# A transformer layer with 32 experts: order of the last weight loads, a rebuilt end, plain activations

## The chip, the cores and the metric
The kernel runs on one core of a Trainium2 chip. The metric is the device time of one execution in microseconds (us). TensorE (PE in the profile), VectorE (DVE), ScalarE (ACT) and GpSimd (POOL) compute; SyncE (SP) does no arithmetic here, it issues nearly all the transfers from the chip's memory.

## The reference
Input x is 256 tokens by 1024, all float32. The layer is

```
mix = three attention groups of x, projected        # first 195 us, not touched by the change
x   = layer_norm(2**0.25 * x + mix) * ln1_g + ln1_b
logits = x @ router_w + router_b ; the 4 best of 32 experts per token, softmax weights w
for each expert e, for its tokens t:
    gu   = x[t] @ w_gate_up[e] + b_gate_up[e]        # 1024 x 2048
    gate = min(gu[:, :1024], 7) ; up = clip(gu[:, 1024:], -7, 7)
    act  = gate * sigmoid(1.702 * gate) * (up + 1)
    ffn[t] += w * (act @ w_down[e] + b_down[e])      # 1024 x 1024
out = layer_norm(2**0.25 * x + ffn) * ln2_g + ln2_b
```

## The kernel before
Every expert's weights are read once: 8 MB for gate and up ("gu") and 4 MB for down ("dn"). SBUF holds two gu buffers (`gu_slot`, one for even experts, one for odd) and one dn buffer (`dn_slot`). A gu is loaded in four chunks of 2 MB, a dn in four of 1 MB. An expert has 64 slots for its tokens. If more tokens chose it, a block of 32 extra slots is run through the same weights (`extra_blocks`). With this input that happens for experts 1 and 15, one block each.

TensorE handles the experts in order. For expert n: 32 gate-up matmuls and 4 for the bias into banks PB4 and PB5 (`gate_up`); then, beside VectorE, the gathering of the next two experts' tokens (after an odd n) or the combine of the last two experts' outputs (`combine`, after an even n); four transposes of `act_sb` (`act_transposes`); 16 down matmuls (`down`). `combine` is a matmul of `CT` (one-hot rows times routing weight, transposed) with `ysb` (outputs of two experts), and adds into banks PB0 to PB3.

VectorE turns gate and up into the activation (`activations`, L1632 to L1638): a minimum and a clip out of PSUM, one multiply with add, a wait for ScalarE's sigmoid, one multiply. The clip results are written interleaved (`by_rows`), since row p of the down weights in SBUF holds four neighbouring rows of the matrix. After the activation VectorE loads the count of extra blocks (`first_extra_slots`, L1682) and, where it is above 0, makes the one-hots of the extra slots (L1656, L1658), for which TensorE waits in `extra_gather`.

The loads stand in one queue, in the order of SyncE's program, and run in that order. SyncE issues chunk c of gu(n+2) when gate-up chunk c of expert n is done (semaphore `guc`, and `xguc` for extra blocks), and chunk c of dn(n+1) when down chunk c of expert n is done (`dn_used`). In the loop (L415) step n issues gu(n+2) and then dn(n+1). For n = 28 and 29 (L423) the two stand the other way round: dn(n+1), then gu(n+2). Last comes dn(31), then ln2_g and ln2_b (L434).

At the end (L1253) TensorE runs gate-up 31, the transposes, down 31 and one combine for experts 30 and 31. Then VectorE, for each half of the tokens (b = 0, 1): residual sum out of PSUM (L1741), statistics (L1513), two normalising passes (L1530, L1535), while GpSimd makes the reciprocal deviation (L520). SyncE writes 128 tokens (512 KB) with one transfer.

Of the kernel before, what the change touches and what calls it, by code (L numbers as in the profile page):

```python
# [22 lines left out]
PAIRS = N_EXPERTS // 2  # L23
SLOTS = 64
# [32 lines left out]
def hybrid_layer(nc, x, w_in, b_in, pos_k, pos_v, w1_k, w2_k, w1_v, w2_v, g_out, w_out, ln1_g, ln1_b,  # L57
                 router_w, router_b, w_gu, b_gu, w_dn, b_dn, ln2_g, ln2_b, out):
    with ExitStack() as ctx:
# [82 lines left out]
        fg, fb = reg_a[:, 0:D], reg_a[:, D:2 * D]  # L142
# [172 lines left out]
        def _(sp_):  # L315
# [98 lines left out]

            with sp.Fori(0, PAIRS - 2) as i:  # L415
                for par in range(2):

                    count_extra_blocks(2 * i + par)
                    next_gu(i, par)
                    next_dn(i, par)  # L420


            for par in range(2):  # L423
                count_extra_blocks(N_EXPERTS - 4 + par)
                next_dn(PAIRS - 2, par)
                next_gu(PAIRS - 2, par)
# [11 lines left out]
            sp.wait_ge(s["outd"], 16 * TB)  # L438
# [92 lines left out]
        def _(act):  # L531
# [205 lines left out]
            sigmoid(1)  # L737
            act_columns(5, 1)
            combine_weights(1)
            act.wait_ge(s["nx_ok"], 1)  # L740
            extra_blocks(0)
            expert_output(0, 1)
            with act.Fori(0, PAIRS - 1) as i:
                sigmoid(2 * i + 2)
                slots_to_sbuf(0, 6, 2 * i + 3)
                act_columns(5, 2 * i + 2)
                slots_to_sbuf(1, 4, 2 * i + 4)
                extra_blocks(2 * i + 1)
                expert_output(1, 2 * i + 2)
                sigmoid(2 * i + 3)  # L750
                act_columns(5, 2 * i + 3)
                combine_weights(i + 2)
                extra_blocks(2 * i + 2)
                expert_output(0, 2 * i + 3)
            sigmoid(N_EXPERTS)
            act_columns(5, N_EXPERTS)
            extra_blocks(N_EXPERTS - 1)
            expert_output(1, N_EXPERTS)
# [3 lines left out]
        def _(pe):  # L762
            mm_, tr = pe.matmul, pe.transpose

# [454 lines left out]
            clear_outputs()  # L1219
            pe.wait_ge(s["ysb_ok"], 1)  # L1220
# [4 lines left out]
            extra_blocks(0, 1, 0, "ct_sb", 1, 0)  # L1225
# [38 lines left out]
        def _(dve):  # L1264
# [455 lines left out]
            with dve.Fori(0, PAIRS - 1) as i:  # L1720
                expert_activations(2 * i + 2)
                next_expert_rows(0, 2 * i + 1)
                first_extra_slots(2 * i + 1)
                extra_blocks(2 * i + 1, 2 * i + 2)
                expert_output(1, 2 * i + 2)
                expert_activations(2 * i + 3)
                next_expert_rows(1, 2 * i + 2)
                first_extra_slots(2 * i + 2)
                extra_blocks(2 * i + 2, 2 * i + 3)
                next_one_hots(i + 1)  # L1730
                expert_output(0, 2 * i + 3)
            expert_activations(N_EXPERTS)
            first_extra_slots(N_EXPERTS - 1)
            extra_blocks(N_EXPERTS - 1, N_EXPERTS)
            expert_output(1, N_EXPERTS)

            dve.wait_ge(s["comb"], PAIRS + 1)
            for b in range(TB):
                for h in range(2):
                    c = slice(512 * h, 512 * h + 512)  # L1740
                    ins = stt(in_order(yf[:, b, c]), by_rows(x_sb[:, b, c]), ALPHA, in_order(PB[2 * b + h][:, :]), ALU.mult,  # L1741
                              ALU.add)
                link(ins)
                half_stats(yf, b, 0)
                link(half_stats(yf, b, 1))
                for h, ins in enumerate(norm(yf, b, TB + b + 1, fg, fb, yf, "ln2_ld")):
                    if h == 1:
                        ins.then_inc(s["fout"], 1)
# [28 lines left out]
```

## Time and profile before

| | us |
|---|---|
| median of 3 runs (lowest, highest) | 1178.83 (1178.04, 1180.24) |
| the profiled execution, its own time | 1177.09 |
| its span, first to last instruction | 1174.9 |
| busy: PE | 1070.8 |
| busy: DVE | 290.6 |
| busy: ACT | 147.7 |
| read from memory | 424.91 MB, mean 363 GB/s |

The profile is of one execution. Its own time is 2.2 us more than its span. Shares of the span say little here, since TensorE and the transfers are both nearly always busy from 285 us on: which of the two is waited for has to be read stretch by stretch. TensorE's granted clock is 1.00 where the engine has its full 2.4 GHz and 0.50 at 1.2 GHz. A float32 matmul is recorded as two matmul entries, so 96 entries are the 16 down and 32 gate-up matmuls that follow each other. "SPq" rows are SyncE's transfer issues.

### The profile page before, as it was taken

To read this page: it belongs to the slowest core of one execution; us is meant where nothing else is said; L and a number is where in the kernel's file an instruction comes from. 1 tells how busy PE (TensorE), PEld (TensorE's weight loads), DVE (VectorE), ACT (ScalarE), POOL (GpSimd) and SP (SyncE) were. 2 spreads that over 40 slices of the span, in tenths; PEclk is the share of its full clock that TensorE was granted. 3 is DMA by queue.
4 is the path that set the end of the run, shared out by engine and by line. 5 is a ranking of instruction groups with operands and counts; after the bars stand their busy time and mean duration, and the time that the engine had idled before them with its cause. 6 is when DMAs were issued, how large, how long until landed. Compare 5 with 4: busy or idle time off the path is not lost.

```text
span 1174.9 us, 14685 instructions
## 1 busy us (share of the span) xinstructions
PE 1070.8 (91%) x5364; PEld 461.1 (39%) x5365; DVE 290.6 (25%) x770; ACT 147.7 (13%) x313; POOL 29.2 (2%) x54
## 2 busy tenths in 40 slices
PE   7999898788999999999999879999999999999984
PEld 6777544332343433323232323434343333333331
DVE  2354654221212121221212212121212121212224
ACT  2043511110010111101010100101010100010100
POOL 3001300000000000000000000000000000000000
PEclk9999997888999999999999989999999999999997
DMA  9723439829999999999999989999999999999980
GB/s 310 269 88 72 184 153 399 343 90 377 426 427 426 427 426 426 427 426 427 426 426 426 426 351 423 426 426 427 426 427 426 427 427 428 424 427 424 426 337 36
DMA packets 48980, 426.32 MB, mean 363 GB/s; under 512 B 5033, under 2 KB 8922, under 8 KB 16154
## 3 DMA queue, kind: packets, MB, share of 16 engines
q1 hardware_dynamic: 48378, 425.37, 87.6%
q10 hardware_dynamic: 576, 0.61, 0.2%
q8 instruction: 16, 0.26, 0.1%
q14 instruction: 10, 0.08, 0.0%
HBM read 424.91 MB, written 1.05 MB: 363 GB/s over the span
## 4 chain that ended last, share of the span: by engine, by line
PE 59%; DMA 29%; DVE 9%; issue 2%; SPq 1%; ACT 1%; DVEq 0%
PE PB L766 57%; DMA WB<-in_w_down_dram 28%; DVE S L1632 2%; DVE S L1633 2%; DVE S L1635 1%; DVE S L1638 1%; PE PB L1123 1%; DMA WB<-in_w_in_dram 1%; DVE S L1530 0%; DVE K L1513 0%; DVE S L1741 0%; DVE S L1496 0%; SPq L330 0%; DVE WB L1415 0%; DVE S L1658 0%
## 5 line engine op out<-in xcount | busy, mean ns | idle before, releaser
L766 PE MATMUL PB<-WB,S 128*64 128x512 f32 (+5 forms) x3456 | 758.4, 595 | 30.8 <-DMA WB<-in_w_down_dram 21.4
L766 PEld LDWEIGHTS PB<-WB,S 128*64 128x64 f32 (+2 forms) x3456 | 255.6, 140 | 513.6 <-issue 440.2
L1632 DVE TENSOR_SCALAR S<-PB 128x512 f32<-128x512 f32 (+1 forms) x34 | 35.5, 1045 | 478.6 <-PE PB L766 478.6
L766 PE MATMUL PB<-S 32*64 32x512 f32 (+5 forms) x464 | 108.1, 586 | 3.2 <-ACT S L700 1.4
L1676 DVE COPY S<-PB 64x512 f32<-64x512 f32 x32 | 21.9, 684 | 264.9 <-PE PB L766 264.9
L704 ACT ACTIVATE S<-S 128x512 f32<-128x512 f32 x32 | 20.2, 630 | 473.0 <-DVE S L1632 473.0
L766 PE MATMUL PB<-S,X 128*128 128x128 f32 x512 | 66.1, 284 | 1.0 <-DVE S L1574 1.0
L766 PEld LDWEIGHTS PB<-S,X 128*128 128x128 f32 x512 | 61.8, 198 | 13.3 <-issue 12.2
L766 PE MATMUL PB<-S,WB 128*128 128x256 f32 (+2 forms) x336 | 60.2, 377 | 1.0 <-ACT S L542 0.5
L766 PEld LDWEIGHTS PB<-S 32*64 32x64 f32 (+5 forms) x464 | 33.1, 147 | 65.2 <-issue 58.0
L766 PEld LDWEIGHTS PB<-S,WB 128*128 128x128 f32 (+1 forms) x336 | 46.5, 170 | 12.3 <-issue 2.1
L720 ACT ACTIVATE S<-PB 64x512 f32<-64x512 f32 x32 | 19.0, 594 | 255.0 <-PE PB L766 255.0
L766 PE MATMUL PB<-WB 128*32 128x128 f32 (+8 forms) x276 | 45.9, 353 | 4.4 <-DVE WB L1461 2.8
L1123 PE MATMUL PB<-K,S 128*128 128x128 f32 x128 | 21.4, 290 | 24.6 <-DVE S L1638 24.6
L766 PEld LDWEIGHTS PB<-WB 128*64 128x64 f32 (+2 forms) x276 | 29.4, 152 | 16.4 <-issue 12.2
L1633 DVE TENSOR_SCALAR S<-PB 128x512 f32<-128x512 f32 (+1 forms) x34 | 35.8, 1053 | 0.1
L1123 PEld LDWEIGHTS PB<-K,S 128*128 128x128 f32 x128 | 13.8, 143 | 41.2 <-DVE S L1638 36.3
L520 POOL TENSOR_TENSOR K<-K 128x1 f32<-128x1 f32 x4 | 3.9, 984 | 997.4 <-DVE K L1526 997.4
L708 ACT ACTIVATE S<-PB 128x512 f32<-128x512 f32 x32 | 19.1, 597 | 66.0 <-PE PB L1123 66.0
L1635 DVE SCALAR_TENSOR_TENSOR S<-S 128x512 f32<-128x512 f32 (+1 forms) x34 | 23.5, 691 | 1.2
L1638 DVE TENSOR_TENSOR S<-S 128x512 f32<-128x512 f32 (+1 forms) x34 | 23.5, 691 | 1.2
L668 ACT ACTIVATE S<-PB 128x512 f32<-128x512 f32 x32 | 19.1, 597 | 15.2 <-PE PB L766 15.2
(208 smaller groups left out, 345.9 us busy)
## 6 DMA issues: line engine op xcount, KB each, us to landing
WB<-in_w_gate_up_dram SPq DMA_DIRECT2D x128, 2048.0 KB, 23.9
WB<-in_w_down_dram SPq DMA_DIRECT2D x128, 1024.0 KB, 21.7
WB<-in_w_in_dram SPq DMA_DIRECT2D x3, 2048.0 KB, 15.8
WB<-in_w_in_dram SPq DMA_DIRECT2D x1, 2144.0 KB, 10.9
WB<-in_w_in_dram SPq DMA_DIRECT2D x2, 1024.0 KB, 10.6
WB<-in_w_out_dram SPq DMA_DIRECT2D x2, 1024.0 KB, 9.7
WB<-in_w_out_dram SPq DMA_DIRECT2D x1, 2048.0 KB, 7.9
WB<-in_w_in_dram SPq DMA_DIRECT2D x1, 1040.0 KB, 12.7
```

What stands on the lines that cost most here:

```text
L520: pool.tensor_tensor(st[:, o + 2:o + 3], st[:, o + 1:o + 2], half[:, 0:1], ALU.pow).then_inc(s["lnp"], 1)
L668: act.activation(xg[:, 4 * h:4 * h + 4, :].rearrange("p k s -> p (k s)"), PB[bank][:, :], ACT.Copy)\
L704: act.activation(act_sb, gt, ACT.Sigmoid, scale=SWIGLU_ALPHA).then_inc(s["sig"], 1)
L708: act.activation(actT[:, :, :].rearrange("p c s -> p (c s)"), PB[bank][:, :], ACT.Copy)\
L720: act.activation(ysb[64 * e:64 * e + 64, 1, :], PB[7][64:128, :], ACT.Copy).then_inc(s["ysb_ok"], 1)
L766: return mm_(o, l, r, start=start, stop=stop, skip_group_check=True)
L1123: ins = tr(PB[5][:, P * c:P * c + P], act_sb[:, P * c:P * c + P], ident)
L1632: ts(by_rows(g), in_order(gate), LIMIT, None, ALU.min).then_inc(s[g_ok], 1)
L1633: ts(by_rows(u), in_order(up), LIMIT, -LIMIT, ALU.min, ALU.max).then_inc(s[clip], 1)
L1635: stt(u, u, 1.0, g, ALU.add, ALU.mult).then_inc(s[upg], 1)
L1638: tt(a, u, a, ALU.mult).then_inc(s[done], 1)
L1676: cp(ysb[64 * e:64 * e + 64, 0, :], PB[7][0:64, :]).then_inc(s["ysb_dv"], 1)
```

## The change
- **Order of loads.** `IN_ORDER = 3`: the order dn(n+1), gu(n+2) begins at n = 24 instead of n = 28.
- **Activations.** The minimum and the clip read PSUM and write SBUF in plain order. The interleaving moves into the transposes: `every_fourth` picks columns m, m+4, m+8, ... of `act_sb` as the matrix to be transposed. It is the operand that is loaded as weights (LDWEIGHTS).
- **Extra slots.** `first_extra_slots(n)` stands before `expert_activations(n+1)` on VectorE. (On TensorE and ScalarE the extra block of expert 0 moves ahead of the first combine; with this input it is empty.)
- **End on TensorE.** In gate-up 31, the outputs of expert 30 are added after chunks 0 and 1 (K = 64 rows), and the combine weights of expert 31 are transposed after chunk 2. After the bias, four matmuls with the identity add 2**0.25 * x (which ScalarE has written out as `x_plain`) into PB0 to PB3. After down 31 the last combine has K = 64 rows: upper and lower rows hold the two halves of the 1024 columns.
- **End on VectorE and SyncE.** Statistics and the first normalising pass read PSUM; both halves' statistics come first, then both norms. Each 128 tokens by 512 columns (256 KB) is written when it is ready.

```diff
-            with sp.Fori(0, PAIRS - 2) as i:
+            with sp.Fori(0, PAIRS - 1 - IN_ORDER) as i:
...
-            for par in range(2):
-                count_extra_blocks(N_EXPERTS - 4 + par)
-                next_dn(PAIRS - 2, par)
-                next_gu(PAIRS - 2, par)
+            with sp.Fori(PAIRS - 1 - IN_ORDER, PAIRS - 1) as i:
+                for par in range(2):
+                    count_extra_blocks(2 * i + par)
+                    next_dn(i, par)
+                    next_gu(i, par)
...
             for b in range(TB):
-                sp.wait_ge(s["fout"], b + 1)
-                sp.dma_start(out[0, P * b:P * b + P, :], yf[:, b, :]).then_inc(s["outd"], 16)
+                for h in range(2):
+                    sp.wait_ge(s["fout"], 2 * b + h + 1)
+                    sp.dma_start(out[0, P * b:P * b + P, 512 * h:512 * h + 512], yf[:, b, 512 * h:512 * h + 512])\
+                      .then_inc(s["outd"], 16)
...
+                    act.activation(x_plain[:, b, c].rearrange("p (q m) -> p q m", q=P),
+                                   x_sb[:, b, c].rearrange("p (m q) -> p q m", q=P), ACT.Copy, scale=ALPHA)\
+                       .then_inc(s["xa"], 1)
+            act.wait_ge(s["ct"], PAIRS + 1)
+            act.activation(CT_last[:, :, :].rearrange("p b t -> p (b t)"), PB[6][:, 0:256], ACT.Copy).then_inc(s["ct_sb"], 1)
...
+            def every_fourth(a, m):
+                return a.rearrange("p (q m) -> p m q", m=4)[:, m, :]
...
-                    ins = tr(PB[5][:, P * c:P * c + P], act_sb[:, P * c:P * c + P], ident)
+                    ins = tr(PB[5][:, P * c:P * c + P], every_fourth(act_sb, c), ident)
...
-            gate_up(1, PAIRS, N_EXPERTS)
-            pe.wait_ge(s["ct_sb"], PAIRS)
+            def outputs_of_30(b):
+                for h in range(2):
+                    mm(acc(b, h)[:, :], CT[0:64, b, :], ysb[0:64, h, :], False, False)
...
+            for c in range(GU_CHUNKS):
+                pe.wait_ge(s_gul[1][c], 16 * PAIRS)
+                gate_up_chunk(c, 1).then_inc(s["guc"], 1)
+                if c == 0:
+                    pe.wait_ge(s["ysb_ok"], N_EXPERTS)
+                    pe.wait_ge(s["ysb_dv"], N_EXPERTS - 1)
+                if c < 2:
+                    outputs_of_30(c)
+                if c == 2:
+                    last_weight_transposes()
+            pe.wait_ge(s["oht"], N_EXPERTS)
+            gate_up_bias(1).then_inc(s["gu"], 1)
+            pe.wait_ge(s["xa"], 1 + 2 * TB)
+            for b in range(TB):
+                for h in range(2):
+                    mm(acc(b, h)[:, :], ident, x_plain[:, b, 512 * h:512 * h + 512], False, False)
...
-            combine()
+            for b in range(TB):
+                for h in range(2):
+                    mm(acc(b, h)[:, :], CT_last[64 * h:64 * h + 64, b, :], y_last[64 * h:64 * h + 64, :], False, True)\
+                        .then_inc(s["comb"], 1)
...
-                ts(by_rows(g), in_order(gate), LIMIT, None, ALU.min).then_inc(s[g_ok], 1)
-                ts(by_rows(u), in_order(up), LIMIT, -LIMIT, ALU.min, ALU.max).then_inc(s[clip], 1)
+                ts(g, gate, LIMIT, None, ALU.min).then_inc(s[g_ok], 1)
+                ts(u, up, LIMIT, -LIMIT, ALU.min, ALU.max).then_inc(s[clip], 1)
...
+                for h in range(2):
+                    dve.wait_ge(s["comb"], PAIRS + 1 + 2 * b + h)
+                    ins = dve.bn_stats(st[:, 12 * b + 6 * h:12 * b + 6 * h + 6], PB[2 * b + h][:, :])
...
+                    ins = stt(yf[:, b, c], PB[2 * b + h][:, :], st[:, o:o + 1], fg[:, c], ALU.subtract, ALU.mult)
...
+                    stt(yf[:, b, c], yf[:, b, c], st[:, o + 2:o + 3], fb[:, c], ALU.mult, ALU.add).then_inc(s["fout"], 1)
```

What this makes of the order, at three places. First SyncE inside the second half of a loop step: before, with a load of gu (L347) after its wait (L405), then dn (L352) after L412, as in every step up to 27:

```order
L347 DMA WB<-in_w_gate_up_dram 128x4096
L361 ISA
L405 ISA
L347 ISA
L347 DMA WB<-in_w_gate_up_dram 128x4096
L412 ISA
L352 ISA
L352 DMA WB<-in_w_down_dram 128x2048
```

and in the changed kernel in steps 24 to 29:

```order
L359 DMA WB<-in_w_down_dram 128x2048
L368 ISA
L419 ISA
L359 ISA
L359 DMA WB<-in_w_down_dram 128x2048
L412 ISA
L354 ISA
L354 DMA WB<-in_w_gate_up_dram 128x4096
```

The four chunks of dn(n+1) now come ahead of the four of gu(n+2) for four more values of n.

Second, VectorE in the loop, second expert of a step: the activation, the next expert's rows, then the count of extra blocks (nx):

```order
L1676 COPY S<-PB 64x512
L1671 REGISTER_ALU
L1632 TENSOR_SCALAR S<-PB 128x128x4
L1633 TENSOR_SCALAR S<-PB 128x128x4
L1635 SCALAR_TENSOR_TENSOR S<-S 128x512
L1638 TENSOR_TENSOR S<-S 128x512
L1615 TENSOR_SCALAR K<-K 128x1
L1611 TENSOR_SCALAR S<-K 128x64
L1679 REGISTER_ALU
L1679 TENSOR_LOAD nx
```

In the changed kernel the end of the one-hots of the extra slots, then the activation:

```order
L1714 TENSOR_SCALAR S<-K 128x32
L1716 TENSOR_SCALAR S<-K 128x32 x4
L1714 TENSOR_SCALAR S<-K 128x32
L1716 TENSOR_SCALAR S<-K 128x32 x4
L1744 UNCONDITIONAL_BRANCH
L1729 REGISTER_ALU
L1690 TENSOR_SCALAR S<-PB 128x512
L1691 TENSOR_SCALAR S<-PB 128x512
L1693 SCALAR_TENSOR_TENSOR S<-S 128x512
L1696 TENSOR_TENSOR S<-S 128x512
L1674 TENSOR_SCALAR K<-K 128x1
L1670 TENSOR_SCALAR S<-K 128x64
```

The one-hots have moved ahead of the wait for the gate-up matmuls, and the two PSUM readers have lost the 128x4 form.

Third, TensorE in expert 31, from its gate-up to the load of the count:

```order
L766 MATMUL PB<-WB,S 64x512 x32
L766 MATMUL PB<-S 64x512 x4
L1123 MATMUL PB<-K,S 128x128 x4
L1191 TENSOR_LOAD nx
L1191 ISA x2
```

and now:

```order
L791 MATMUL PB<-WB,S 64x512 x8
L791 MATMUL PB<-S 128x512 x2
L791 MATMUL PB<-WB,S 64x512 x8
L791 MATMUL PB<-S 128x512 x2
L791 MATMUL PB<-WB,S 64x512 x8
L1288 MATMUL PB<-K,WB 128x128 x2
L791 MATMUL PB<-WB,S 64x512 x8
L791 MATMUL PB<-S 64x512 x4
L791 MATMUL PB<-WB,K 128x512 x4
L1148 MATMUL PB<-K,S 128x128 x4
L1216 TENSOR_LOAD nx
```

Ten instructions stand before the four transposes that did not: four for expert 30, two transposes, four for the residual.

## Rows read from the trace of the kernel before

**Rows 1.** The page's part 2, 40 equal slices of the span.
```profile
GB/s 310 269 88 72 184 153 399 343 90 377 426 427 426 427 426 426 427 426 427 426 426 426 426 351 423 426 426 427 426 427 426 427 427 428 424 427 424 426 337 36
```

**Rows 2.** The chain of waits: start us, us, what.
```profile
1039.86 1.96 PE PB L766 x8
...
1069.41 16.73 PE PB L766 x80
```

**Rows 3.** The timeline, expert 30: start, us, engine, line, operation, [idle before <-releaser].
```profile
1113.02 1.04 DVE L1632 TENSOR_SCALAR S<-PB 128x512 f32<-128x512 f32 x1 [14.09 <-PE PB L766]
...
1116.46 0.66 PE L1123 MATMUL PB<-K,S 128*128 128x128 f32 x4 [0.74 <-DVE S L1638]
...
1118.13 20.82 PE L766 MATMUL PB<-WB,S 128*64 128x512 f32 x96
```

**Rows 4.** The timeline, SyncE's issues of dn(29) and of dn(31).
```profile
1064.09 7.71 SPq L352 DMA_DIRECT2D WB<-in_w_down_dram  x4
...
1120.20 5.47 SPq L352 DMA_DIRECT2D WB<-in_w_down_dram  x4
```

**Rows 5.** Stretches near the end; last columns: granted clock, DMA share, GB/s.
```profile
1135.00:1140.00 5.00, 4.97 (x28) 1.27 (x24) 0.00 (x0) 0.00 (x0) 0.00 (x0) 1.00 0.95 386
...
1145.00:1150.00 5.00, 4.70 (x14) 1.47 (x16) 0.00 (x0) 0.25 (x1) 0.00 (x0) 0.57 0.02 3
```

**Rows 6.** The timeline, expert 31 and the end.
```profile
1143.53 1.08 PE L1123 MATMUL PB<-K,S 128*128 128x128 f32 x4 [3.57 <-DVE S L1638]
...
1145.31 9.06 PE L766 MATMUL PB<-WB,S 128*64 128x512 f32 x32 [0.69 <-ACT S L708]
...
1155.25 3.67 PE L766 MATMUL PB<-S 128*128 128x512 f32 x8 [0.88 <-DVE S L1676]
...
1158.96 1.96 DVE L1741 SCALAR_TENSOR_TENSOR S<-X,PB 128x512 f32<-128x512 f32 x2 [3.85 <-PE PB L766]
1160.95 1.29 DVE L1513 BATCH_NORM_STATS2 K<-S 128x6 f32<-128x512 f32 x2
...
1162.59 1.40 DVE L1530 SCALAR_TENSOR_TENSOR S<-S,K,WB 128x512 f32<-128x512 f32 x2
...
1165.47 6.73 SPq L437 DMA_DIRECT2D out_dram<-S  x2
...
1170.42 1.41 DVE L1535 SCALAR_TENSOR_TENSOR S<-S,K,WB 128x512 f32<-128x512 f32 x2
```

**Rows 7.** The timeline, extra blocks of expert 1 (first two rows) and of expert 15.
```profile
256.69 9.62 PE L766 MATMUL PB<-WB,S 128*32 128x512 f32 x64 [0.47 <-ACT S L683]
...
278.51 1.99 PE L766 MATMUL PB<-S 64*128 64x512 f32 x8 [0.71 <-ACT S L700]
...
673.12 0.60 ACT L668 ACTIVATE S<-PB 128x512 f32<-128x512 f32 x1 [0.30 <-PE PB L766]
...
675.28 1.07 PE L766 MATMUL PB<-X,S 128*32 128x256 f32 x16 [2.19 <-DVE S L1658]
...
677.76 7.07 PE L766 MATMUL PB<-WB,S 128*32 128x512 f32 x64 [0.47 <-ACT S L683]
...
689.57 0.69 PE L1175 MATMUL PB<-K,S 128*128 128x128 f32 x2 [3.74 <-DVE S L1638]
```

**Rows 8.** Stretches of 6 us around the two extra blocks.
```profile
282.00:288.00 6.00, 6.00 (x30) 2.01 (x28) 0.44 (x1) 0.44 (x1) 0.00 (x0) 1.00 0.75 221
...
676.00:682.00 6.00, 5.02 (x50) 1.53 (x46) 0.00 (x0) 0.77 (x2) 0.00 (x0) 1.00 0.68 244
...
700.00:706.00 6.00, 6.00 (x30) 2.01 (x28) 0.00 (x0) 0.00 (x0) 0.00 (x0) 1.00 0.69 231
```

**Rows 9.** Groups by line and form (VectorE, 280 to 1140 us), and the page's part 5.
```profile
L1632 DVE TENSOR_SCALAR S<-PB 128x512 f32<-128x512 f32 x29 | 30.4, 1047 | 408.5 <-PE PB L766 408.5
...
L1676 DVE COPY S<-PB 64x512 f32<-64x512 f32 x30 | 20.5, 684 | 239.8 <-PE PB L766 239.8
...
L1123 PEld LDWEIGHTS PB<-K,S 128*128 128x128 f32 x128 | 13.8, 143 | 41.2 <-DVE S L1638 36.3
```

More of the change, by code:

```diff
@@ L141, in hybrid_layer @@
         yf = S2[:, 0:TB * D].rearrange("p (b d) -> p b d", b=TB)
-        fg, fb = reg_a[:, 0:D], reg_a[:, D:2 * D]
+        take = carver(reg_a)
+        fg, fb = take(D), take(D)
+        x_plain = take(TB * D, b=TB, d=D)
+        y_last = take(512)
+        CT_last = take(TB * P, b=TB, t=P)
+        ohw_last = take(TB * P, b=TB, s=P)
         K = sb("K", 1202)
@@ L757, in _ @@
             extra_blocks(N_EXPERTS - 1)
-            expert_output(1, N_EXPERTS)
+            act.wait_ge(s["dn_used"], N_EXPERTS * DN_CHUNKS)
+            act.activation(y_last[64:128, :], PB[7][64:128, :], ACT.Copy).then_inc(s["ysb_ok"], 1)
         @block.tensor
@@ L1251, in _, with last_weight_transposes @@
                 down(0, i + 2, 2 * i + 3)
[L1253 to L1254 removed]
+            def outputs_of_30(b):
+                for h in range(2):
+                    mm(acc(b, h)[:, :], CT[0:64, b, :], ysb[0:64, h, :], False, False)
+            def last_weight_transposes():
+                pe.wait_ge(s["ohs"], PAIRS + 2)
+                pe.wait_ge(s["ct_sb"], PAIRS)
+                for b in range(TB):
+                    ins = tr(PB[6][:, P * b:P * b + P], ohw_last[:, b, :], ident)
+                ins.then_inc(s["ct"], 1)
+            for c in range(GU_CHUNKS):
[11 more added lines that the diff above has]
+            pe.wait_ge(s["xa"], 1 + 2 * TB)
+            for b in range(TB):
+                for h in range(2):
+                    mm(acc(b, h)[:, :], ident, x_plain[:, b, 512 * h:512 * h + 512], False, False)
+            pe.wait_ge(s["ct_sb"], PAIRS + 1)
             act_transposes(N_EXPERTS)
@@ L1259, in _ @@
             pe.wait_ge(s["ysb_dv"], N_EXPERTS)
-            combine()
+            for b in range(TB):
+                for h in range(2):
+                    mm(acc(b, h)[:, :], CT_last[64 * h:64 * h + 64, b, :], y_last[64 * h:64 * h + 64, :], False, True)\
+                        .then_inc(s["comb"], 1)
         @block.vector
@@ L1731, in _ @@
                 expert_output(0, 2 * i + 3)
+            t = N_EXPERTS - 1
+            for b in range(TB):
+                for j in range(2):
+                    ins = ts(ohw_last[:, b, 64 * j:64 * j + 64], iota_s, posm[:, t, b:b + 1], wts[:, t, b:b + 1], ALU.is_equal,
+                             ALU.mult)
+            ins.then_inc(s["ohs"], 1)
+            first_extra_slots(t)
             expert_activations(N_EXPERTS)
[L1733 to L1737, printed above, removed]
+            extra_blocks(t, N_EXPERTS)
+            dve.wait_ge(s["dn_used"], N_EXPERTS * DN_CHUNKS)
+            cp(y_last[0:64, :], PB[7][0:64, :]).then_inc(s["ysb_dv"], 1)
             for b in range(TB):
+                o = 24 + 4 * b
+                for h in range(2):
+                    dve.wait_ge(s["comb"], PAIRS + 1 + 2 * b + h)
+                    ins = dve.bn_stats(st[:, 12 * b + 6 * h:12 * b + 6 * h + 6], PB[2 * b + h][:, :])
+                link(ins)
+                link(dve.bn_aggr(st[:, o:o + 2], st[:, 12 * b:12 * b + 12]))
+                ts(st[:, o + 1:o + 2], st[:, o + 1:o + 2], LN_EPS, None, ALU.add).then_inc(s["lnstat"], 1)
+            dve.wait_ge(s["ln2_ld"], 32)
+            for b in range(TB):
+                o = 24 + 4 * b
                 for h in range(2):
                     c = slice(512 * h, 512 * h + 512)
-                    ins = stt(in_order(yf[:, b, c]), by_rows(x_sb[:, b, c]), ALPHA, in_order(PB[2 * b + h][:, :]), ALU.mult,
-                              ALU.add)
+                    ins = stt(yf[:, b, c], PB[2 * b + h][:, :], st[:, o:o + 1], fg[:, c], ALU.subtract, ALU.mult)
                 link(ins)
[L1744 to L1748, printed above, removed]
+                dve.wait_ge(s["lnp"], TB + b + 1)
+                for h in range(2):
+                    c = slice(512 * h, 512 * h + 512)
+                    stt(yf[:, b, c], yf[:, b, c], st[:, o + 2:o + 3], fb[:, c], ALU.mult, ALU.add).then_inc(s["fout"], 1)
     return nc
```

18 lines of the change are left out of this document (10 added, 8 removed).

## The prediction, made before the changed kernel ran

> **What bounds the kernel now.** I read four views, in this order. The 40 slices first [rows 1]: the transfers run at 426 or 427 GB/s nearly everywhere from slice 10 on. One slice is lower (351, from 675 us), and slice 8 (from 235 us) has 90. So the weight stream is full, with gaps at two places.
>
> The chain of waits next: between 476 and 651 us, and between 896 and 1069 us, it is a row of transfers, one expert every 29.5 us (1039.86 to 1069.41 [rows 2]). From 1069.41 on it is TensorE and VectorE. An expert then takes 27.1 us (transposes at 1116.46 [rows 3], the next at 1143.53 [rows 6]). Three such experts lie between 1069.41 and the end of down 31 at 1154.4, so 1069.41 is the last chunk of dn(28).
>
> SyncE's issues and the stretches tell why [rows 4, 5]. dn(31) is issued at 1120.2, but the stream still moves 386 GB/s until 1140: what is left after 1069.41 (dn 29, gu 30, dn 30, gu 31, dn 31) is 29.4 MB, or 69 us at 427 GB/s. dn(31) has landed near 1138, down 31 ends at 1154.4. The load order of the loop brings gu(n+2) ahead of dn(n+1), which is needed first; when the stream ends, TensorE is 16 us behind it.
>
> The last view is the timeline of the end [rows 6]: from down 31's end at 1154.4 to the end of the span at 1174.9 are 20.5 us, nearly all on VectorE.
>
> **The order of the loads.** At 427 GB/s a gu takes 19.67 us (4.92 a chunk), a dn 9.84 (2.46 a chunk). dn(24) landed at 1069.4 - 4 x 29.52 = 951.3. Now seven dn and six gu follow in order of use: dn(31) lands at 951.3 + 68.9 + 118.0 = 1138.2, as before, gu(31) 9.8 before that, at 1128.4, and gu(30) 29.5 earlier, at 1098.9. From the last chunk of its gu to the end of its down, TensorE needs: 0.2 to start (an estimate), one gate-up chunk 3.46 (20.82 / 6, by 16 of 96 entries [rows 3]), bias 1.1, the wait for the activation 2.8 (next part), transposes and what follows until down 1.67 (1116.46 to 1118.13 [rows 3]), down 6.9 (20.82 / 3). That is 16.1. So down 30 ends at 1098.9 + 16.1 = 1115.0 (1125 before).
>
> Does the stream run dry? dn(n+1) is issued while down n runs; ahead of it then stands gu(n+1), up to 19.7 us long. Where before changes its order, dn(29) was issued from 1064.1 on [rows 4] with only dn(28) ahead of it, and no gap shows in the chain. At n = 24 TensorE also waits for the stream, so it is the same transition. I take no gap. The order would cost something only if TensorE were more than about 15 us behind there.
>
> Expert 31: four chunks 13.8; two times two matmuls for expert 30, which share their rows of the array and so don't pair: 4 x 0.86 = 3.4 (3.67 for four of full height [rows 6], 1.99 for four in pairs [rows 7]: both ends kept); two transposes 0.3; bias 1.1: 1115.0 + 18.6 = 1133.6. Then the residual, 3.5 by the same row. It fills the 3.57 us for which TensorE waited here [rows 6]; VectorE's chain (2.8) ends before it. Transposes and ScalarE's copy 1.35: 1138.4. Down 31 took 9.06 for 32 entries after that idle wait, with the clock at 0.57 [rows 5], against 6.9 at 1.00. With no idle wait I take 6.9 (9.1 is the other end). Down 31 ends at 1145.4, not 1154.4: **-9.0** (-6.5 to -10.5). ScalarE's four residual copies and the copy of the weights have 18 us before they are needed.
>
> **The activations.** L1632 takes 1047 ns, a plain copy out of PSUM 684 [rows 9]. Two of them: 0.72 us less per expert, so 2.8 instead of 3.5. TensorE waits 0.74 there [rows 3]; most of that goes, and then its gather or combine (2.8 to 2.9) is what lasts. In the stretches bound by transfers this is worth nothing. It counts in the 2.8 above and in the extra blocks.
>
> The other side is the transposes: their weight loads (143 ns each, four per expert [rows 9]) now read every fourth float32. No row of before shows a strided weight load. Below: nothing. Above: VectorE's scattered form costs (1047 - 684) / 512 = 0.7 ns per element, which on 128 columns is 0.09 us per load, 0.36 per expert. I take 0.2 per expert, and as the far end four times the load, 1.7 per expert. In transfer-bound stretches 0.2 is hidden; at the end it costs **+0.2**.
>
> Against this stands a rule of the Trainium skill, "Advanced Engine Details and Errata", section on memory cachelines: SBUF has lines of 16 bytes, and an access that goes to a new line each time pays. Every fourth float32 is exactly a new line. It gives no price, so it moves only the chance of the first rival; L1632 agrees in direction with its 1.5 times, if writes behave as reads.
>
> **The extra blocks** are where gaps in the stream can be closed. For expert 15 TensorE waits 2.19 us for the one-hots until 675.28 [rows 7]. Now they are made before gate-up ends. What is late next is ScalarE's copy of bank PB4, which starts at the gather's end and takes 0.60; the gather ends 0.6 earlier. It would end at 673.1, so 2.2 earlier than 675.28. Within the block TensorE waits 3.74 for an activation with two scattered reads [rows 7]: 0.7 less. That is 2.9, less 0.4 for strided transposes. The clock is a further term: the 64 entries took 9.62 in expert 1 and 7.07 in expert 15 [rows 7], so up to 2.5 in the first, and up to 2 in each after the long wait. I take 2.0 for expert 1 and 0.7 for expert 15.
>
> Does the stream gain it? gu(17) is held up by the extra gate-up, dn(16) by down 15. The two stretches lack (427 - 244) x 6 / 427 = 2.6 and 2.8 us [rows 8], so 5.4 at most; I take 3.2. For expert 1 the stretch 282 to 288 lacks 2.9 and restarts when down 1 does; the stream before it (gu 3) restarts 2.2 or more earlier too, so the cap is above 5. I take 4.5. After both gaps the stream is full, so all later landings move: **-7.7** (-5 to -10.3).
>
> **The tail.** After down 31: copies 0.85 (1154.4 to 1155.25). Combine in pairs 1.99 instead of 3.67; the first pair is done at half. Statistics start at 2.0 after down's end: 1.3 for two [rows 6], from PSUM the same I assume, then 0.4 to the next pass (1160.95 + 1.29 to 1162.6); for both halves of the tokens 5.5. Four pairs of passes: 1.45 out of PSUM, 1.4 the others: 5.7, so 11.2. GpSimd's step of the first half is hidden beside the second's statistics. Before, this was 17.4 (1171.83). The two residual passes of 1.96 and the last half's wait are what goes. The last transfer is 256 KB instead of 512; from VectorE's end to the span's end were 3.1 us, I take 3.0. Tail 14.2 instead of 20.5: **-6.3** (-5.3 to -7.3).
>
> **Sum.** Span 1174.9 - 9.0 + 0.2 - 7.7 - 6.3 = 1152.1. The profiled execution's own time would be 1177.09 - 22.8 = 1154.3, and the median of the runs, 1.7 above it, 1178.83 - 22.8 = **1156.0**.
>
> **Rivals.**
> - *Dear strided loads.* At 1.7 us per expert TensorE needs 27.9 per expert, still less than the stream's 29.5. But the lag of the extra blocks is barely paid back by expert 24, and each late expert adds. I worked it through expert by expert: 18 us worse, 1174. At 1.0 it is 5 worse, 1161. The skill's rule speaks for it, the nearest row (0.36) against it.
> - *The extra blocks give nothing* (the gaps stay, because the requests come no earlier than the stream's restart): 1163.7. Against it: both gaps end about 2 us after requests that hang on the extra block.
> - *The new order gives nothing*: TensorE waits in gate-up instead of in down, and a gap opens since dn(25) is issued late: 1165. Against it: dn(29) [rows 4] did the same without a gap.
> - *Slower than before.* The same strided loads, priced above 1.85 per expert, or 0.6 us for a load that took 0.14. Then TensorE is still behind at expert 24, and in the new order dn(25) isn't even asked for until down 24 runs, while nothing stands behind dn(24): the stream stops for 6 to 10 us there. At 2.1 per expert: 32 worse than the forecast, 1188.
> - *The two last gains overlap with something not seen*, leaving the time as it was: nothing in the rows speaks for it.
>
> **Chances.** Forecast 0.72; extra blocks nothing 0.09; order nothing 0.08; dear loads but still faster 0.06; no change 0.02; slower 0.03. A measurement of this kernel can tell about 0.2% (2.4 us) from no change. Faster 0.95, within 0.2% 0.02, slower 0.03. The ends of the terms give 1151 to 1161 for the forecast alone; the range for 8 in 10 is 1151.5 to 1164.5, which takes in the second rival.
>
> **What would show it.** In the changed profile: down 31's 32 entries take 6.9 at clock 1.00 and end near 1138; transfers end near 1131; the chain's waits for dn end at expert 24 and turn into short waits for gu chunks. The transposes' four entries stay near 0.66, weight loads near 0.14 to 0.23. The stretches at 676 and 700 us lack less than half of what they lacked. VectorE takes 11 us from down 31 to its last pass. The prediction is wrong if the transposes take over 2 us per expert, if the stream shows a gap after dn(24), or if down 31 still starts over 15 us after gu(31) has landed.

## The result, and the profile of the changed kernel

| | before | changed |
|---|---|---|
| median of four runs each | 1178.52 us (1178.04 to 1180.24) | 1150.92 us (1150.05 to 1152.26) |
| ratio, 95% interval | | 0.9765 (0.9747 to 0.9784) |
| profiled execution: own time, span | 1177.09, 1174.9 | 1150.07, 1147.9 |
| span until down 1 starts | 280.4 | 271.0 |
| last chunk of dn(24) landed | 951.3 | 938.9 |
| down 31 ends | 1154.4 | 1134.5 |
| from there to the end of the span | 20.5 | 13.4 |

The forecast was 1156.0 with a range of 1151.5 to 1164.5. The kernel came out 27.6 us faster, where 22.8 were forecast, and 0.6 us below the range.

The slices of the changed kernel, which answer to [rows 1]:

```profile
GB/s 309 263 110 74 148 132 395 400 149 399 423 426 425 427 427 426 427 427 425 427 427 425 429 417 399 427 427 426 427 427 426 427 421 426 427 425 427 427 425 157
```

The low value at the first extra block is 149 instead of 90 and the one at expert 15 is 399 instead of 351. At the end 425 stands up to the last slice but one, where before had 337 and 36. In the changed kernel the same work comes earlier: down 1 by 9.5 us, the extra gate-up of expert 15 by 11.4, down 15 by 12.3. So the stretches that answer to [rows 8] lie as much earlier (last column GB/s):

```profile
272.54:278.54 6.00, 6.00 (x30) 2.01 (x28) 0.44 (x1) 0.44 (x1) 0.00 (x0) 1.00 0.90 292
664.63:670.63 6.00, 5.03 (x50) 1.53 (x46) 0.00 (x0) 0.77 (x2) 0.00 (x0) 1.00 0.98 384
687.74:693.74 6.00, 6.00 (x30) 2.01 (x28) 0.00 (x0) 0.00 (x0) 0.00 (x0) 1.00 0.86 313
```

Measured against 427 GB/s they lack 1.9, 0.6 and 1.6 us, where before lacked 2.9, 2.6 and 2.8. The gaps are smaller, not closed. The chain of waits, answering to [rows 2] (start us, us, what):

```profile
911.61 27.26 DMA WB<-in_w_down_dram
938.92 19.56 PE PB L791 x104
...
1049.23 37.53 DMA WB<-in_w_gate_up_dram
1086.81 4.72 PE PB L791 x24
```

The waits for dn end with dn(24) at 938.92. After that only chunks of gate-up weights are waited for, 0.65 us in gate-up 29 and twice 1.24 in gate-up 30. The end of the changed kernel, answering to [rows 6] (TensorE and VectorE in one timeline):

```profile
1112.05 1.98 PE L791 MATMUL PB<-S 64*128 64x512 f32 x4
...
1122.51 3.70 PE L791 MATMUL PB<-WB,K 128*128 128x512 f32 x8
1122.65 0.69 DVE L1690 TENSOR_SCALAR S<-PB 128x512 f32<-128x512 f32 x1 [17.84 <-PE PB L791]
...
1126.05 0.63 PE L1148 MATMUL PB<-K,S 128*128 128x128 f32 x4
...
1127.37 7.09 PE L791 MATMUL PB<-WB,S 128*64 128x512 f32 x32 [0.69 <-ACT S L718]
1135.34 1.99 PE L791 MATMUL PB<-WB 64*128 64x512 f32 x8 [0.88 <-DVE WB L1801]
1136.47 1.30 DVE L1806 BATCH_NORM_STATS2 K<-PB 128x6 f32<-128x512 f32 x2 [1.28 <-PE PB L791]
...
1143.95 1.41 DVE L1820 SCALAR_TENSOR_TENSOR S<-S,K,WB 128x512 f32<-128x512 f32 x2
```

The last eight combine entries go in pairs, 1.99 us. TensorE goes straight from gate-up 31 through the residual into the transposes: the 3.57 us wait is gone, and the 32 entries of down 31, with 0.69 of idle time ahead of them, take 7.09 instead of 9.06. A stretch within them, answering to [rows 5], has the granted clock at 1.00 (2.4 GHz), against 0.57 before:

```profile
1129.00:1134.00 5.00, 5.00 (x26) 1.58 (x22) 0.00 (x0) 0.00 (x0) 0.00 (x0) 1.00 0.00 0
```

VectorE's last pass ends at 1145.4, 10.9 us after down 31.

What had not been forecast is at the start. TensorE before, from the weight transposes of expert 0 to down 1:

```profile
221.94 23.67 PE L766 MATMUL PB<-WB,S 128*64 128x512 f32 x96 [6.06 <-issue]
...
253.95 1.07 PE L766 MATMUL PB<-X,S 128*32 128x256 f32 x16 [2.23 <-DVE S L1658]
...
280.42 10.09 PE L766 MATMUL PB<-WB,S 128*64 128x512 f32 x46
```

and changed:

```profile
211.12 4.04 PE L791 MATMUL PB<-S 128*128 128x256 bf16 x15
217.58 0.70 PE L791 MATMUL PB<-S 128*128 128x512 f32 x1 [2.41 <-issue]
...
219.43 22.09 PE L791 MATMUL PB<-WB,S 128*64 128x512 f32 x96 [0.26 <-ACT S L718]
...
247.86 1.07 PE L791 MATMUL PB<-X,S 128*32 128x256 f32 x16 [0.82 <-ACT S L678]
...
250.34 7.07 PE L791 MATMUL PB<-WB,S 128*32 128x512 f32 x64 [0.47 <-ACT S L693]
...
270.96 19.53 PE L791 MATMUL PB<-WB,S 128*64 128x512 f32 x90
```

Before, TensorE stood idle for 6.06 us ahead of down 0 and waited for nothing that the profile names. The only thing between the transposes and down 0 in the program is the extra block of expert 0, which is empty. In the changed kernel that block stands ahead of the first combine, the idle time is 2.41, and it lies in the combine, ahead of the last of its eight entries (the x15 row holds the eight matmuls that clear the outputs and the first seven entries of the combine). Down 1 starts 9.5 us earlier, and the waits for dn(24) end 12.35 us earlier, where 7.7 were forecast.

### The profile page after: what moved, and what is told of

It is laid out like the page before. It is cut to its first block, busy times and chain, and to the rows that moved or that the text cites. A ratio compares the mean times of both kernels' runs of the same rounds, so it can differ in the third digit from the quotient of the medians.

```text
span 1147.9 us, 14752 instructions
## 1 busy us (share of the span) xinstructions
PE 1073.4 (94%) x5382; PEld 463.7 (40%) x5383; DVE 265.1 (23%) x770; ACT 152.4 (13%) x318; POOL 28.3 (2%) x54
## 4 chain that ended last, share of the span: by engine, by line
PE 62%; DMA 30%; DVE 5%; issue 1%; SPq 1%; ACT 1%; DVEq 0%
PE PB L791 59%; DMA WB<-in_w_down_dram 26%; DMA WB<-in_w_gate_up_dram 3%; PE PB L1148 1%; DMA WB<-in_w_in_dram 1%; DVE S L1693 1%; DVE S L1696 1%; DVE S L1690 1%; DVE S L1691 1%; DVE S L1555 0%; DVE S L1815 0%; SPq L337 0%; DVE WB L1474 0%; DVE S L1589 0%; DVE K L1806 0%
## 5 line engine op out<-in xcount | busy, mean ns | idle before, releaser
L1690 DVE TENSOR_SCALAR S<-PB 128x512 f32<-128x512 f32 (+1 forms) x34 | 23.5, 691 | 482.1 <-PE PB L791 482.1
L791 PE MATMUL PB<-WB 128*32 128x128 f32 (+9 forms) x284 | 48.1, 362 | 5.3 <-DVE WB L1520 2.8
L791 PEld LDWEIGHTS PB<-WB 128*64 128x64 f32 (+3 forms) x284 | 30.3, 153 | 18.7 <-issue 12.6
L1148 PEld LDWEIGHTS PB<-K,S 128*128 128x128 f32 x128 | 18.1, 210 | 17.2 <-DVE S L1696 16.4
L1148 PE MATMUL PB<-K,S 128*128 128x128 f32 x128 | 23.7, 308 | 1.4
L1691 DVE TENSOR_SCALAR S<-PB 128x512 f32<-128x512 f32 (+1 forms) x34 | 23.2, 682 | 0.1
```

The source lines that it names most:

```text
L791: return mm_(o, l, r, start=start, stop=stop, skip_group_check=True)
L1148: ins = tr(PB[5][:, P * c:P * c + P], every_fourth(act_sb, c), ident)
L1690: ts(g, gate, LIMIT, None, ALU.min).then_inc(s[g_ok], 1)
L1691: ts(u, up, LIMIT, -LIMIT, ALU.min, ALU.max).then_inc(s[clip], 1)
```

## The experiments

All times of an experiment are set against the kernel before on the same chip; its ratio is then set against the changed kernel's 0.9765. One thousandth is 1.2 us. The difference of two such ratios is uncertain by about 0.0028, 3.3 us, so small terms are read from the traces.

### The start

**x0_back**: the changed kernel, with the empty block where it was (TensorE's lines; ScalarE's move with them).

```diff
-            extra_blocks(0, 1, 0, "act", 1, 0)
             pe.wait_ge(s["ysb_ok"], 1)
...
             weight_transposes()
+            extra_blocks(0, 1, 0, "ct_sb", 1, 0)
             down(0, 1, 1, first=True)
```

> The changed kernel, with TensorE's and ScalarE's empty extra block of expert 0 put back to where it stood, between the transposes of the weights and the first matmuls of down 0. Theory (code loading): before, TensorE stood idle for 6.06 us there with nothing that the profile names, and for 2.41 us after; down 0 then starts about 2.5 us later again, and its and gate-up 1's matmuls lose about 1.6 us more to the lower clock: 1.0039 or 4 to 5 us above the changed kernel, 1155 to 1156. Rival: the earlier start of down 0 comes from elsewhere and the wait for the one-hots hides it: 0 to 0.5 us, 1151 to 1151.5.

1154.05 us, ratio 0.9796 (0.9777 to 0.9816): 3.7 above the changed kernel. TensorE's timeline:

```profile
223.45 22.14 PE L791 MATMUL PB<-WB,S 128*64 128x512 f32 x96 [5.89 <-issue]
...
275.05 15.24 PE L791 MATMUL PB<-WB,S 128*64 128x512 f32 x70
```

The idle time is back at 5.89, and down 1 starts 4.1 later. Of the 4.1, 1.3 stand ahead of the edit, since the clearing of the outputs starts at 212.40 for 211.12: counted from there it is 2.8. The rival falls.

**x0_alone**: the kernel before, with only that move (the same lines, and ScalarE's). The block then stands ahead of the first combine, as in the changed kernel, not behind a part of down 0, as the expectation has it.

> The kernel before, with only the empty extra block of expert 0 moved behind the first token tile of down 0 on TensorE and ScalarE. Theory (code loading): 4 to 5 us faster, 1174, or only 2 us where the wait for the one-hots of expert 1's extra block, which is still there, takes back what the earlier start gives. Rival: nothing, 1178.5.

1174.71 us, ratio 0.9971 (0.9960 to 0.9981), 3.4 faster than before. The wait for the one-hots (2.23) stayed and took nothing back:

```profile
216.14 0.70 PE L766 MATMUL PB<-S 128*128 128x512 f32 x1 [1.64 <-issue]
...
276.25 13.95 PE L766 MATMUL PB<-WB,S 128*64 128x512 f32 x64
```

Down 1 starts 4.2 earlier, 3.9 counted from the clearing of the outputs.

**slots_alone**: the kernel before, with only VectorE's one-hots of the extra slots moved.

```diff
+                first_extra_slots(2 * i + 1)
                 expert_activations(2 * i + 2)
                 next_expert_rows(0, 2 * i + 1)
-                first_extra_slots(2 * i + 1)
```

> The kernel before, with only VectorE's and GpSimd's work on the first slots of the extra blocks moved ahead, so that TensorE no longer waits for the one-hots at experts 1 and 15. Theory: 2.0 at expert 1, 2.9 at expert 15, and 2.5 more at expert 1 if the extra gate-up then runs at 1.00 of the clock instead of 0.68: 4.9 to 7.4 us faster, 1171 to 1173.5. Rival (the waits are taken over by another wait, for the slots' positions or a load): 0 to 2 us faster.

1172.79 us, ratio 0.9948 (0.9929 to 0.9967), 6.1 faster. What is late next is the copy that the prediction named, for 0.81 us, and the extra gate-up ran at the full clock here:

```profile
251.17 1.07 PE L766 MATMUL PB<-X,S 128*32 128x256 f32 x16 [0.81 <-ACT S L668]
...
253.65 7.07 PE L766 MATMUL PB<-WB,S 128*32 128x512 f32 x64 [0.47 <-ACT S L683]
...
276.10 14.38 PE L766 MATMUL PB<-WB,S 128*64 128x512 f32 x66
```

Down 1 starts 4.3 earlier. 1.4 of them lie in down 0 and gate-up 1 (22.30 for 23.67), which the edit doesn't touch, and the extra down matmuls took 1.6 more (6.49 for 4.93). What the edit itself gives is 1.4 of wait and 2.6 in the extra gate-up. So the 4.5 us forecast for expert 1 are about what this part gives by itself, and the empty block's 4.2 come on top. With 0.7 for the activation within the block these make 9.2 of the 9.5.

**x0_gone**: the changed kernel, the line `extra_blocks(0, 1, 0, "act", 1, 0)` deleted on TensorE.

> The changed kernel without TensorE's share of expert 0's extra block, which is empty with this input: it leaves out the computation of tokens beyond the first slots of expert 0. Theory: the idle 2.41 us that stay at the jump over this block are code loading, and go: 1.5 to 3 us faster, 1148 to 1149.5. Rival: the idle time belongs to something else at this place (the queue of TensorE, a transfer) and stays: 0 to 0.5 us, or the fetch comes at the next place and takes as much there.

1147.72 us (1147.12 to 1148.20), ratio 0.9744 (0.9722 to 0.9766). No idle time stands in the combine, and down 1 starts at 268.77, 2.2 earlier than in the changed kernel, and 3.6 earlier counted from the clearing of the outputs. By the ratio alone the 2.5 us would not be told from nothing, but the two ranges don't meet, since the changed kernel's fastest run took 1150.05. The rival falls.

**x0_early**: the block still further ahead.

```diff
             gate_up(0, 1, 1)
+            extra_blocks(0, 1, 0, "act", 1, 0)
             expert_weight_transposes()
             clear_outputs()
-            extra_blocks(0, 1, 0, "act", 1, 0)
```

> The changed kernel with TensorE's empty extra block of expert 0 put further ahead, between gate-up 0 and the 16 matmuls that clear the outputs (its outputs, of which this input has none, would be cleared: it leaves them out). Theory (code loading that runs beside matmuls already fetched): 4.5 us more of cover, the idle 2.41 us vanish, 2 to 3 us faster, as without the block: 1147.7 to 1149. Rival: the idle time comes a fixed count of instructions behind the jump, now in the middle of the clearing, and stays on the path: 1150.5 to 1151.5.

1147.47 us, ratio 0.9736 (0.9710 to 0.9762): 3.4 below the changed kernel and the shortest of all. It is no version to use, since it would lose expert 0's extra tokens where there are any.

```profile
210.33 4.47 PE L791 MATMUL PB<-S 128*128 128x256 bf16 x16
...
215.96 20.82 PE L791 MATMUL PB<-WB,S 128*64 128x512 f32 x96 [0.47 <-ACT S L718]
```

The x16 row holds the eight matmuls of the clearing and the combine's eight entries; the expectation calls all 16 the clearing. The block is in the program and no idle time is left. So it is not the block by itself that costs, but how much TensorE has to do while something is fetched.

The branch over the block can be seen by itself. Its line in the trace (least, median and longest duration in ns, then its start), on TensorE's sequencer, in the kernel before, in the changed kernel and in x0_early:

```profile
L1193 PEldq COMPARE_BRANCH  x1: 6784/6784/6784, 215.0 to 215.0; - x1
```

```profile
L1218 PEldq COMPARE_BRANCH  x1: 370/370/370, 210.8 to 210.8; - x1
```

```profile
L1218 PEldq COMPARE_BRANCH  x1: 367/367/367, 207.3 to 207.3; - x1
```

Before, the branch itself lasted 6.78 us (6.62 in x0_back), to just ahead of down 0. In the changed kernel it took 0.37, and seven entries of the combine went before TensorE stopped. So what is missing there lies behind the branch's target, not at it. What stays nearly the same is the time from the start of the branch to the first entry behind the idle time: 6.95 us before, 6.81 changed, 6.79 in x0_back, and between 6.0 and 7.2 in all twelve kernels that have this idle time. The earlier the branch comes, the more of that time is work. In x0_early it starts at 207.29; 6.8 us later is 214.1, and the entries of the x16 row run until 214.8.

The view of the transfers points to what is waited for. The queue that carries instructions moves 16 packets in the whole execution of the changed kernel, and 15 in x0_gone. From the pages of the two:

```profile
q8 instruction: 16, 0.26, 0.1%
```

```profile
q8 instruction: 15, 0.25, 0.1%
```

That is 16 KB a packet. One of them starts at 219.1 before, 214.9 changed, 220.5 in x0_back and 211.2 in x0_early; in x0_gone none starts between 209 and 219. TensorE goes on at 221.94, 217.58 and 223.45, that is 2.7 to 2.9 us after it in each of the first three; in x0_early 213.9 would be that time, when the x16 row still runs. The Trainium skill, "Advanced Engine Details and Errata", section on the ISA cache, says that instructions are held in lines of 16 KB, 256 instructions; the packet's size agrees. That the jump leaves such a line is read from this; no run changed the size of the block.

### The last experts

**order_old**: the changed kernel with `IN_ORDER = 1` instead of 3.

> The changed kernel with the last six experts' loads in the old order (the count of experts loaded in order of use back to 1). Theory: the down weights of expert 31 come ahead of its gate-up weights again, TensorE waits for the last gate-up chunks at the end, and 7 to 9 us come back: 1158 to 1160. Rival: the order is worth nothing once the other parts are in, since the same bytes have to come: 0 to 1 us, 1151 to 1152.

1159.82 us, ratio 0.9847 (0.9829 to 0.9864), 9.7 above the changed kernel. TensorE's timeline:

```profile
1056.78 15.67 PE L791 MATMUL PB<-WB,S 128*64 128x512 f32 x72 [0.56 <-DMA WB<-in_w_down_dram]
...
1135.63 7.09 PE L791 MATMUL PB<-WB,S 128*64 128x512 f32 x32 [0.69 <-ACT S L718]
```

The waits for dn go on to 1056.78 (dn(28)) and down 31 starts 8.3 later than 1127.37. The rival falls.

**order_alone**: the kernel before with the order only (`IN_ORDER = 3` and SyncE's loop of the change).

> The kernel before with only the order of the last loads changed (three experts in order of use). Theory: 7 us faster, 1171.5 (6 to 8.5); the last activations wait for nothing but their own gate-up. Rival: the gain needs the other parts as well (the combine of 30 beside the last loads), and the order by itself gives 0 to 3 us, 1175.5 to 1178.5.

1173.16 us (1167.04 to 1175.48, 11 runs), ratio 0.9960 (0.9946 to 0.9974): 4.7 faster, less than expected. The profile is of the fastest of the 11, so it shows where TensorE waits, not where the typical run lost:

```profile
1126.05 3.65 PE L768 MATMUL PB<-WB,S 128*64 128x512 f32 x16 [2.31 <-DMA WB<-in_w_gate_up_dram]
1134.29 0.63 PE L1125 MATMUL PB<-K,S 128*128 128x128 f32 x4 [3.57 <-DVE S L1640]
1135.61 8.64 PE L768 MATMUL PB<-WB,S 128*64 128x512 f32 x32 [0.69 <-ACT S L710]
```

TensorE waits 0.82 and 2.31 for chunks of gate-up 31. With the new end the outputs of 30 stand in these waits. Part of the order's worth may hang on that: 9.7 with the new end, 4.7 without, though the two differ by little more than they are uncertain. In this profile down 31 starts 9.7 earlier than before, but dn(24) has already landed 3.5 earlier (947.78 for 951.27), ahead of everything that the edit touches. That leaves 6.2, and 0.4 in down 31, close to the 7 of the theory. Why the median isn't nearer to 7 stays open.

**end_old**: the kernel before with every part but the new end (the order, the empty block's place, the one-hots' place and the plain activations together).

> The kernel before with every part of the change but the new end: order of the last loads, expert 0's empty block ahead, first extra slots ahead, activations in order of the banks. The outputs of 30, the combine of 31, the residual and the norm stand as in the kernel before. Theory: the end after down 31 takes 20.5 us again for 13.4, and down 31 goes at the lower clock, some 1.5 us more: 7 to 9 us above the changed kernel, 1158 to 1160. Rival (the new end also lets the last loads or gate-up 31 come earlier): 10 us and more, over 1161; or under 5 us where the new end's gain is mostly the clock.

1160.17 us, ratio 0.9843 (0.9810 to 0.9877), 9.2 above the changed kernel.

```profile
1118.37 3.65 PE L772 MATMUL PB<-WB,S 128*64 128x512 f32 x16 [2.20 <-DMA WB<-in_w_gate_up_dram]
...
1126.00 0.72 PE L1129 MATMUL PB<-K,S 128*128 128x128 f32 x4 [2.96 <-DVE S L1644]
...
1127.45 8.78 PE L772 MATMUL PB<-WB,S 128*64 128x512 f32 x32 [0.73 <-ACT S L710]
...
1137.10 3.67 PE L772 MATMUL PB<-S 128*128 128x512 f32 x8 [0.87 <-DVE S L1682]
```

Down 31 starts at 1127.45, against 1127.37: with the order in place the new end gains nothing ahead of it. Down 30 started 1.1 later here (1097.17 for 1096.10), so counted from there the new end even costs 1.0. The 3.96 us of outputs lie where TensorE waits 1.25 and 2.20 for gu(31), the 3.70 of the residual where it waits 2.96 for VectorE. Down 31 itself takes 1.7 more behind the idle wait (8.78 for 7.09, with a mean granted clock of 0.80), and the end behind it 20.5 for 13.4. These two are the 8.9 us by which the spans differ.

**no_residual**: the changed kernel without the residual's matmuls.

```diff
-            for b in range(TB):
-                for h in range(2):
-                    mm(acc(b, h)[:, :], ident, x_plain[:, b, 512 * h:512 * h + 512], False, False)
```

> The changed kernel without the four matmuls by the identity that add the residual ahead of down 31; the residual is left out of the result. Theory: they take 3.70 us beside a wait of TensorE for the last weights and for the activations of gate-up 31, and keep its clock up; without them down 31 goes at the lower clock, 9.1 us for 7.09, and the whole is 0 to 2 us slower. Rival: they stand on the path to the end, and the whole is 0.7 to 3.5 us faster.

1150.50 us, ratio 0.9773 (0.9750 to 0.9797): no change that can be measured.

```profile
1125.10 0.72 PE L1148 MATMUL PB<-K,S 128*128 128x128 f32 x4 [2.96 <-DVE S L1693]
1126.51 8.72 PE L791 MATMUL PB<-WB,S 128*64 128x512 f32 x32 [0.69 <-ACT S L718]
```

Down 31 starts 0.9 earlier, 0.4 of it already there when down 30 starts, and takes 1.6 more, at a mean granted clock of 0.81 for 1.00. The residual on TensorE pays for itself: what it lasts beyond VectorE's chain comes back by the clock.

### The activations

**act_old**: the changed kernel with the scattered activations and contiguous transposes. What is scattered is the writing into SBUF (`by_rows`); PSUM is read in order (`in_order`) in both. The extra blocks' transposes and the clip change in the same way.

```diff
-                    ins = tr(PB[5][:, P * c:P * c + P], every_fourth(act_sb, c), ident)
+                    ins = tr(PB[5][:, P * c:P * c + P], act_sb[:, P * c:P * c + P], ident)
...
-                ts(g, gate, LIMIT, None, ALU.min).then_inc(s[g_ok], 1)
+                ts(by_rows(g), in_order(gate), LIMIT, None, ALU.min).then_inc(s[g_ok], 1)
```

> The changed kernel with the old scattered activations and the old contiguous transposes. Theory: the activation on the path takes 1047 ns again for 691, the four transposes 0.66 us for 0.75 and their weight loads 143 ns for 210; over the experts in which TensorE, not the loads, sets the pace this leaves 1.4 to 2 us in all: 1152.3 to 1153. Rival A (strided weight loads are dear and the shorter activation was hidden): 0.5 to 3 us faster, 1148 to 1150.5. Rival B (loads set the pace wherever the two differ): no change.

1154.70 us, ratio 0.9803 (0.9782 to 0.9825): 4.5 above the changed kernel (about 1.2 to 7.8 with the uncertainty), twice what was expected; rivals A and B fall. The groups by form of the changed kernel, VectorE and weight loads, answering to [rows 9]:

```profile
L1690 DVE TENSOR_SCALAR S<-PB 128x512 f32<-128x512 f32 x30 | 20.8, 692 | 427.1 <-PE PB L791 427.1
...
L1148 PEld LDWEIGHTS PB<-K,S 128*128 128x128 f32 x128 | 18.1, 210 | 17.2 <-DVE S L1696 16.4 <-issue 0.7
```

and the four transposes of one expert in act_old:

```profile
1044.14 0.66 PE L1148 MATMUL PB<-K,S 128*128 128x128 f32 x4 [0.75 <-DVE S L1696]
```

The strided loads cost 67 ns each and 0.09 us for four transposes (0.75 for 0.66); the waits of 0.65 to 0.75 for VectorE are gone. In the trace 3.2 of the 4.7 us by which down 31 starts later are there when down 1 starts, 0.8 more when down 15 does, and the last 0.8 behind it. Of the 3.2, 1.0 stands before the first activation and is no doing of the edit. Another 0.3 is a longer idle time at the jump over expert 0's block (2.74 for 2.41), 0.6 a wait of the transposes of expert 1 for the activation, and 0.7 the wait within the extra block (3.75 for 3.07). The last 0.7 are slower matmuls behind that wait (5.74 for 5.28 in the extra down alone). So about 3.4 of the 4.7 are the edit's.

### How far the order can be carried

**order_7** and **order_14**: the changed kernel with `IN_ORDER = 7` and `14`.

> The changed kernel with the loads in order of use from expert 16 on instead of from expert 24 on. Theory: TensorE lags the loads by 10 us at both places, the loads never wait for a buffer, and only the bytes in all count: -0.5 to +0.5 us, 1150.5 to 1151.5. Rival A: the two waits of 1.24 us for chunks of gate-up 30 go too, 1 to 2.5 us faster. Rival B: the loads stop for want of a free buffer after the extra block of expert 15, 1 to 5 us slower.

> The changed kernel with the loads in order of use from expert 2 on. There TensorE lies furthest behind, since the extra block of expert 1 has just put it back. Theory (a buffer of down weights comes free later than its loads would go, and the order of use makes the queue wait for it): the stream has a gap of 2 to 10 us, 1153 to 1161. Rival: the lag is gone before it matters, 1150.5 to 1151.5.

1166.23 us, ratio 0.9890 (0.9864 to 0.9916), and 1172.18 us, ratio 0.9941 (0.9922 to 0.9961): 14.7 and 20.7 above the changed kernel. My theory for order_7 was wrong, its rival B right in kind and three times too small. The theory for order_14 was right in kind, with 2 to 10 us, half of what came. Stretches of order_7 and SyncE's issues:

```profile
702.00:708.00 6.00, 6.00 (x30) 2.01 (x28) 0.00 (x0) 0.00 (x0) 0.00 (x0) 1.00 0.16 66
708.00:714.00 6.00, 5.91 (x27) 2.19 (x24) 3.00 (x6) 0.63 (x1) 0.00 (x0) 1.00 0.00 0
714.00:720.00 6.00, 6.00 (x29) 2.10 (x29) 1.94 (x10) 0.98 (x2) 0.00 (x0) 1.00 0.29 71
```

```profile
690.86 31.95 SPq L359 DMA_DIRECT2D WB<-in_w_down_dram  x8
723.16 2.30 SPq L354 DMA_DIRECT2D WB<-in_w_gate_up_dram  x4
```

The switch falls behind the extra block of expert 15, when TensorE lags furthest. Eight chunks of dn then stand in a row at SyncE, and the last four can't go before down 16 gives their buffers free; gu stands behind them, though its own buffers are free. In these 18 us the stream moves 0.8 MB where the changed kernel moves 7.8, which is 16 us at 427 GB/s. In order_14 the same happens behind expert 1's extra block (eight chunks of dn issued over 32.07 us from 273.54 on, 0 GB/s from 287 to 293). At expert 24, where the change switches, the same eight chunks of dn stand in a row, issued over 37.22 us from 904.23 on, and gu(26) behind them from 941.80. But there TensorE is waiting for the stream (0.45 to 0.78 us ahead of each chunk of down 24), loads issued earlier are still coming in, and nothing stops: from 918 to 966 us no stretch of 6 us is under 414 GB/s.

## Why the prediction was wrong, point by point

- **The failed step: the extra blocks, at the start.** "I take 4.5" for expert 1 measured 9.4, and the step as a whole 12.35 against 7.7, beyond its own far end of 10.3. The 4.5 itself was near (4.3 in slots_alone), by some luck: 1.4 us gained in down 0 and gate-up 1 and 1.6 lost in the extra down, neither of which I had in the sum, nearly cancel there. Missing was the empty extra block of expert 0, which the change moves on TensorE and which I costed at nothing, without saying what would hide it. It gives 4.2 and 4.1 at down 1 in x0_alone and x0_back, 3.9 and 2.8 counted from the clearing of the outputs, through an idle time of 6.06 us that stood in the trace of before. I had read that timeline from 256 us on and never asked for the chain's "issue" ahead of down 0.
- *Expert 15*: 3.2 forecast, 2.9 measured. The wait of 2.19 became 0.81, the 3.74 became 3.07. Its clock can't be priced: 64 entries took 7.07 in some executions and 8.7 to 9.4 in others, whichever version.
- *The cap on the gaps*: at expert 15 the two stretches lacked 5.4 us and lack 2.2 now, so 3.2 were closed, what I took. At expert 1 the gap of slice 8 shrank too (90 to 149 GB/s). All later landings moved by the whole 12.35.
- *The order and expert 31*: 8.8 forecast with the strided loads, 7.6 measured. The step "seven dn and six gu follow in order of use" held, as did "I take no gap" at expert 24. Too small were the outputs of 30 (1.98 twice, not 3.4 in all), the residual (3.70 for 3.5) and down 31 (7.09 for 6.9): 1.0 of the 1.2. That down 31 would go at the full clock once nothing idles ahead of it is what end_old and no_residual show from the other side (8.78 and 8.72, behind a wait of 2.96).
- *"more than about 15 us behind"*: the change shows no gap at expert 24, but order_7 shows that the term exists and can cost 15 us. The 15 us of lag as a threshold were not tested.
- *The strided loads*: 0.2 per expert forecast, 0.09 measured, nearer to the lower end. The scattered reads that I counted within the extra block are scattered writes; the 0.7 that I took for them is what the wait lost (3.74 to 3.07). The rule on lines of 16 bytes of the Trainium skill ("Advanced Engine Details and Errata", section on memory cachelines) agrees in direction, 210 ns against 143; the two rivals on dear loads fall.
- *The tail*: 6.3 forecast, 7.1 measured. VectorE's part was near (10.9 for 11.2, with no wait in it from the statistics on); from its end to the end of the span are 2.5, not 3.0.

The sum: 9.4 + 2.9 + 7.6 + 7.1 = 27.0, the difference of the spans. Against it I had 4.9 too little at the start, 0.3 too much at expert 15, 1.2 too much in the order, 0.8 too little in the tail. The last three come to 0.7 together, so the miss of the time is the start's.

## What to carry to other kernels

- Ask of a profile's "issue" idle time on the path as of any wait, and of a moved block what its jump costs even when it is empty. Here some 6 to 7 us passed from the branch to the entry that had to be fetched; a jump costs least where that time is filled with work.
- When one queue carries two streams of loads, switch to the order of use only where the consumer is waiting for the queue. The same edit gave 9.7 us at expert 24 and cost 15 at expert 16.
- Work moved into a wait ahead of the last matmuls can pay twice: once for what it replaces (the end behind down 31 is 7.1 us shorter) and once by the clock of what follows (1.6 to 1.7 us).

## What the runs showed of the hardware

- A jump over an empty block of about 136 matmul entries (counted in expert 15's) kept TensorE idle for 5.4 to 6.1 us with down 0 right behind it, 1.6 to 2.7 with a combine behind it, and not at all with 4.9 us of work behind it. The branch itself was recorded with 6.1 to 6.8 us in the first case and 0.37 or 0.38 in the other two.
- Weight loads of the transposes that read every fourth float32 took 210 ns for 143. Activations of 512 float32 written with a step took 1047 ns, written in order 692.
- Matmuls of 64 rows in the same half of the array took 1.98 us for four entries, in opposite halves 1.99 for eight.
- Down 31 took 7.09 us behind matmuls and 8.6 to 9.1 behind an idle wait of 3 to 3.6 us.
